# Two-layer attention trunk: softmax with queries on the partitions, scaled on GpSimd and transposed, in place of key-major scores with running sums from TensorE

## The chip, the core and the metric

The kernel runs on one core of a Trainium2 chip. The metric is the device time in microseconds (us) of one execution. The kernel before takes 1517.91 us, the median of three runs (1515.63 to 1521.51). Everything is float32; the large products are made of two or three TensorE passes over a "high" part (the value rounded to the fp32r format) and a "low" part (the rest).

## The reference

Two layers over 640 tokens (128 context tokens, tile 0, and 512 latent tokens, tiles 1 to 4), width 1024. Per layer one input projection feeds three branches; the outputs are projected, gated, merged, projected again and normalised. The change touches the attention of branches A and B only. Both have 8 query heads and 2 key/value heads of 64 columns.

```python
def dense_gqa(q, k, v, n_kv, sink=None):          # branch A; latent queries see 4 latent tiles + 1 cached tile
    s = einsum('bqkgd,blkd->bkgql', q * d**-0.5, k)
    ...                                            # branch B: the sink is one more column of s
    p = softmax(s, axis=-1)                        # without the sink's column afterwards
    return einsum('bkgql,blkd->bqkgd', p, v)

def window_gqa(q, k, v, k_ctx, v_ctx, sink):       # branch B; |i - j| <= 128, plus the cached tile, plus the sink
    s_band = where(valid, einsum(q, kband), -1e30)
    p = softmax(concatenate([s_band, s_ctx, s_sink], -1), -1)
    return p_band @ vband + p_ctx @ v_ctx
```

Context queries (tile 0) see context keys alone.

## The kernel before

**Groups and steps.** Attention runs group by group. A group is one key/value head with one tile of 128 queries, so 4 query heads and 512 (head, query) columns; `GROUPS` lists 10 of them, the context tile last. A step is one key tile of a group. Branch A has 8 groups of 5 steps and 2 of one step, 42 in all. Branch B has groups of 3 or 4 key tiles and one more step for the sink (`SINK`), 40 steps in all, 30 of them with keys. There are two layers, so 144 steps with keys and 20 with the sink.

**What a group does.** First it needs the row maximum of each query. `S` (L1043, L1045) forms the scores with queries on the partitions, one head at a time over all its latent keys in one bank (128 x 512 or 128 x 384; in B with a mask product, L1050), and the cached tile of branch A in one more unit with the four heads side by side. VectorE takes the maxima (L1586, L1589), combines them with each other or the sink (L1595 to L1602). `row` (L1057) transposes the 128 x 4 maxima; VectorE writes them, negated, into rows 96 to 99 of a copy `q_m` of the queries (L1612, L1614). Then each step `ST` forms the scores again, this time with keys on the partitions: L1071, and L1072, in which rows 96 to 99 of `k_lo` hold ones so that the maximum is subtracted inside the product; in B a mask product (L1076) where the tile needs it. ScalarE takes the exponential from the bank (L1296) and rounds it to `p_hi` (L1298), GpSimd makes `p_lo` (L1792). `PV` adds three products (L1092, L1093, L1095) to the output bank: high values times `p_hi`, low values times `p_hi`, high values times `p_lo`. The stationary tile of values is 64 columns of values next to 64 columns of ones, so the other half of the bank gathers the sum of the exponentials. For the sink, `ST` writes a diagonal tile of exponentials (L1291) and `PV` multiplies it with ones (L1089, L1095). `O` (two halves) takes the reciprocal of 64 x 256 sums (L1633) and multiplies (L1636, twice). `og`, `oh`, `ol` apply the gate and split the result (L1798, L1311, L1803).

**Order.** All engines walk one list, `ORDER`, each in its own program order, and wait on semaphores. `attention()` writes the list for a branch: a step, the `S` units and `row`s of later groups spread between, the `PV` of three steps back, and a chunk of filler: gate products over 640 tokens (L910) that do not depend on the attention. In A the filler is the gate tiles `z` 2 to 7, in 8 chunks each of 6 matmuls of 320 columns; in B it is `c` and `u`, 6 chunks each of 8 matmuls. In B `c` goes through ScalarE with Silu, which needs another table than Exp. `S` and `row` share banks 0 and 1, `ST` banks 2 and 3, `O` banks 4 and 5, filler banks 6 and 7. `with_splits` puts the preparation of weight tiles between: ScalarE rounds one (L1138), GpSimd makes its low part (L1764).

**Buffers that the change touches.** `p_f`, `p_hi`, `p_lo` (three buffers of 128 x 512 each), `o_inv`, `q_m`, `es_d`, `es_f`, `top_r`, and `vv`, the values with their columns of ones.

## Time and profile before

| | us |
|---|---|
| median of 3 runs | 1517.91 |
| the profiled execution, its own time | 1520.94 |
| its span, first to last instruction | 1519.1 |
| TensorE busy in the span | 1445.8 |
| VectorE, ScalarE, GpSimd busy | 796.1, 587.9, 771.7 |
| mean granted TensorE clock | 0.986 |

TensorE has work for all but 73.3 us of the span. A matmul's duration on the page includes its way through the pipe, so the durations of neighbours overlap; what one costs is the distance between two starts, which the timeline gives. PE stands for TensorE, PEld for its weight loads, DVE for VectorE, ACT for ScalarE, POOL for GpSimd. Line numbers are those of the kernel before.

### The profile page before, as it was taken

Reading aid. Unit: us, or ns where it says so; the run is one execution under the profiler, and the core shown is the slowest. Engines: PE = TensorE matmul, PEld = TensorE weight load, DVE = VectorE, ACT = ScalarE, POOL = GpSimd, SP = SyncE. Lnnn points to the kernel's source line nnn. Section 1 sums busy time; section 2 is a strip of 40 time slices with the busy share of each in tenths; the row PEclk is TensorE's granted clock in tenths of the full one; section 3 lists DMA queues with packets and bytes.
Section 4 is the critical chain, followed back from the end, with each engine's and each line's share of the span. In section 5 each row is a group of like instructions: output and inputs, shape, how many; then the busy total and the mean of one; then the engine's idle time right before and its main releaser. Section 6 shows DMA issues by size and latency. Waiting matters only on the chain.

```text
span 1519.1 us, 21747 instructions
## 1 busy us (share of the span) xinstructions
PE 1445.8 (95%) x8776; PEld 1306.1 (86%) x8776; DVE 796.1 (52%) x1164; ACT 587.9 (39%) x934; POOL 771.7 (51%) x554
## 2 busy tenths in 40 slices
PE   5999999999998999999979999998999999999996
PEld 3898889889887888999868988897988879999985
DVE  4675676452677520312784747764436775022157
ACT  4334564233764311213243346542357632222140
POOL 2454676323676443344674557753246755443443
PEclk9999999999999999999999999999999999999998
DMA  8412000212000443444320220012110013215221
GB/s 336 126 56 74 29 28 21 90 47 83 28 29 28 132 156 122 141 159 139 124 98 28 88 70 15 29 56 73 56 57 28 29 53 113 76 62 198 96 99 70
DMA packets 36756, 126.90 MB, mean 84 GB/s; under 512 B 5040, under 2 KB 5680, under 8 KB 36656
## 3 DMA queue, kind: packets, MB, share of 16 engines
q1 hardware_dynamic: 29952, 108.54, 21.3%
q10 hardware_dynamic: 6704, 16.97, 3.1%
q8 instruction: 70, 1.15, 0.3%
q14 instruction: 30, 0.25, 0.1%
HBM read 119.73 MB, written 5.77 MB: 83 GB/s over the span
## 4 chain that ended last, share of the span: by engine, by line
PE 87%; DVE 5%; POOL 3%; issue 2%; ACT 2%; DVEq 0%; POOLq 0%; ACTq 0%
PE ps L910 46%; PE ps L858 7%; PE ps L860 7%; PE ps L859 7%; PE ps L1045 3%; PE ps L1043 2%; PE ps L1095 2%; PE ps L1072 2%; PE ps L1071 2%; PE ps L1092 2%; PE ps L1093 2%; PE ps L927 1%; POOL w_lo L1764 1%; DVE o_inv L1633 1%; PE ps L1102 1%
## 5 line engine op out<-in xcount | busy, mean ns | idle before, releaser
L1764 POOL TENSOR_TENSOR w_lo<-raw,w_hi 128x1024 fp32r<-128x1024 f32 x148 | 360.1, 2440 | 359.0 <-ACT w_hi L1138 358.7
L910 PE MATMUL ps<-h_hi,w_hi 128*128 128x320 f32 x1280 | 299.3, 315 | 18.4 <-DVE g_c L1645 8.0
L910 PE MATMUL ps<-h_hi,w_lo 128*128 128x320 f32 x1280 | 292.6, 310 | 0.0
L910 PE MATMUL ps<-h_lo,w_hi 128*128 128x320 f32 x1280 | 292.6, 310 | 0.0
L1792 POOL TENSOR_TENSOR p_lo<-p_f,p_hi 128x512 fp32r<-128x512 f32 x164 | 211.9, 1296 | 139.0 <-ACT p_hi L1298 138.2
L910 PEld LDWEIGHTS ps<-h_hi,w_hi 128*128 128x128 f32 x1280 | 217.3, 189 | 39.3 <-DVE g_c L1645 9.8
L910 PEld LDWEIGHTS ps<-h_lo,w_hi 128*128 128x128 f32 x1280 | 215.9, 189 | 2.2
L910 PEld LDWEIGHTS ps<-h_hi,w_lo 128*128 128x128 f32 x1280 | 215.6, 189 | 2.2
L1138 ACT ACTIVATE w_hi<-raw 128x1024 fp32r<-128x1024 f32 x148 | 152.8, 1051 | 92.1 <-DMA raw<-in_weights 53.7
L1589 DVE TENSOR_REDUCE top<-ps 128x1 f32<-128x512 f32 (+1 forms) x128 | 83.7, 658 | 144.7 <-PE ps L1050 105.0
L1660 DVE TENSOR_TENSOR gy<-ps,sg 128x640 f32<-128x640 f32 x32 | 26.4, 824 | 241.2 <-PE ps L910 241.1
L1633 DVE RECIPROCAL o_inv<-ps 64x256 f32<-64x256 f32 x80 | 140.2, 1752 | 15.3 <-PE ps L1095 10.4
L1296 ACT ACTIVATE p_f<-ps 128x512 f32<-128x512 f32 x144 | 86.1, 598 | 133.0 <-PE ps L1095 117.8
L858 PE MATMUL ps<-w_hi,h_hi 128*128 128x512 f32 (+1 forms) x360 | 130.5, 362 | 4.0 <-POOL w_lo L1764 2.6
L860 PE MATMUL ps<-w_hi,h_lo 128*128 128x512 f32 (+1 forms) x360 | 128.5, 357 | 0.0
L859 PE MATMUL ps<-w_lo,h_hi 128*128 128x512 f32 (+1 forms) x360 | 128.4, 357 | 0.0
L1336 ACT ACTIVATE sg<-ps,pack 128x640 f32<-128x640 f32 x32 | 25.4, 795 | 207.7 <-PE ps L910 207.6
L1298 ACT ACTIVATE p_hi<-p_f 128x512 fp32r<-128x512 f32 x164 | 103.7, 632 | 5.2
L910 PE MATMUL ps<-o_hi,w_hi 128*128 128x320 f32 x384 | 91.4, 320 | 6.9 <-DVE rot_s L1385 6.0
L1807 POOL TENSOR_TENSOR merge<-merge,gy 128x640 f32<-128x640 f32 x32 | 51.2, 1601 | 82.3 <-DVE gy L1660 82.3
L910 PE MATMUL ps<-o_lo,w_hi 128*128 128x320 f32 x384 | 88.6, 312 | 0.0
L910 PE MATMUL ps<-o_hi,w_lo 128*128 128x320 f32 x384 | 88.6, 312 | 0.0
(180 smaller groups left out, 2599.2 us busy)
## 6 DMA issues: line engine op xcount, KB each, us to landing
raw<-in_weights SPq DMA_DIRECT2D x190, 512.0 KB, 3.4
raw_more<-in_weights SPq DMA_DIRECT2D x10, 512.0 KB, 10.6
x<-in_x_sample ACTq DMA_DIRECT2D x6, 512.0 KB, 8.0
x_mid<-x ACTq DMA_DIRECT2D x5, 512.0 KB, 2.6
x<-x_mid ACTq DMA_DIRECT2D x5, 512.0 KB, 6.5
y_sample<-x SPq DMA_DIRECT2D x3, 512.0 KB, 2.6
pack<-in_pack ACTq DMA_DIRECT2D x2, 528.0 KB, 4.8
x<-in_x_sample SPq DMA_DIRECT2D x2, 512.0 KB, 4.9
```

The lines of the kernel that those rows point to most:

```text
L858: pe.matmul(out, st_hi, mv_hi, start=start, stop=False)
L859: pe.matmul(out, st_hi, mv_lo, start=False, stop=False)
L860: return pe.matmul(out, st_lo, mv_hi, start=False, stop=stop)
L910: last = pe.matmul(ps[:, s + half, 0:HALF], w[:, u % RING, cols], acts[:, k, half * HALF:(half + 1) * HALF], start=k == 0 and part == 0, s ...
L1138: did(act.activation(w_hi[:, n % RING, :], raw_tile(r), ACT.Copy), hi_made)
L1296: did(act.activation(p_f[:, n % 3, :], ps[:, s, :], ACT.Exp), drained[s])
L1298: did(act.activation(p_hi[:, n % 3, :], p_f[:, n % 3, :], ACT.Copy), p_hi_made)
L1589: did(dve.tensor_reduce(top[:, c, 0, i:i + 1], ps[:, s, 0:n * P], axis=AX.X, op=ALU.max), drained[s])
L1633: after(did(dve.reciprocal(o_inv[0:HD, cols], ps[sums, b, cols])))
L1764: did(pool.tensor_tensor(w_lo[:, n % RING, :], raw_tile(r), w_hi[:, n % RING, :], ALU.subtract), w_ready)
L1792: did(pool.tensor_tensor(p_lo[:, n % 3, :], p_f[:, n % 3, :], p_hi[:, n % 3, :], ALU.subtract), p_lo_made)
L1807: did(pool.tensor_tensor(merge[:, j, :], merge[:, j, :], gy[:, j % 2, :], ALU.add), merged)
```

## The change

Scores are formed once, with queries on the partitions (`S`). ScalarE takes the exponential of a whole head directly from that bank, with the negated maximum as the per-partition bias, and has the row sum accumulated at the same time (`ex`); the sink becomes one more exponential of a 128 x 1 column. VectorE adds the partial sums and takes the reciprocal of a 128 x 1 column (`iv`), GpSimd multiplies the head's row of exponentials by it. The step is now `T`: four transposes of 128 x 128 on TensorE. ScalarE rounds the transposed bank to `p_hi`, VectorE makes the low part (`pl`). `PV` has two products: the stationary tile of values is 64 high columns next to 64 low columns, so the upper half of the bank gathers the low part; ScalarE copies it out and VectorE adds both (`O`, once per group). The steps of the sink, the second scores, `row`, `q_m` and the columns of ones are gone; so is row 96 to 99 of `k_lo` (the scores take 96 rows). In branch A the cached unit comes first and is copied to `cached`. `p_f` holds two whole groups. The lag from step to `PV` is 2, not 3; the filler of A begins one `z` tile earlier and eight chunks of it stand between the first `S` units, in B one gate tile of `b` is filler too. A split is held back between the last `S` of a group and its last `iv`.

```diff
+def p_place(g):
+    return (g % 2, 0, g - 2) if g < 2 * T - 2 else (0, g - (2 * T - 2), 2 * T - 4)
...
-def attention(l, br, filler, last_filler, lag, row_ahead, score_ahead):
+def attention(l, br, first_filler, filler, last_filler, lag, ahead):
...
+        holder = p_place(g)[2]
+        start = -1 if holder < 0 else first[holder + 1] - 1
+        end = max(first[g] - ahead, start)
+        ahead_of_heads = len(units) > GRP and holder >= 0
         for i, e in enumerate(units):
+            n = i - ahead_of_heads
+            at = start - 1 if n < 0 else start + (end - start + 1) * n // (len(units) - ahead_of_heads)
+            scores[at].append(e)
+            exps[at].append(("ex", *e[1:]))
+            if score_units(br, g)[e[4]] != "cache":
+                inverses[at if at < 0 else at + 1].append(("iv", *e[1:]))
...
     for n, (g, i) in enumerate(steps):
-        out.append(("ST", l, br, g, i))
-        out.extend(early[n])
+        out.append(("T", l, br, g, i))
+        out.extend(scores[n])
+        out.append(("pl", l, br, g, i))
+        out.extend(inverses[n])
         tick()
         if n >= lag:
             product(n - lag)
         fill()
+        out.extend(exps[n])
...
-    out.extend(flat(attention(l, "a", filler[:-5], filler[-5:], 3, 2, 4)))
+    out.extend(flat(attention(l, "a", filler[:8], filler[8:-5], filler[-5:], 2, 3)))
...
-    out.extend(flat(attention(l, "b", filler[:-3], filler[-3:], 3, 2, 4)))
+    out.extend(flat(attention(l, "b", filler[:9], filler[9:-3], filler[-3:], 2, 3)))
...
+        def p_part(br, g):
+            buf, behind, _ = p_place(g)
+            n = len(group_slots(br, g)) * P
+            return by_head(p_f[br][:, buf, behind * BW:behind * BW + GRP * n])
...
@@ TensorE
-                        pe.matmul(ps[:, s, :], k_hi[:, kv, key], q_t[:, heads, tokens], start=True, stop=False)
-                        last = pe.matmul(ps[:, s, :], k_lo[0:TOP_ROW + GRP, kv, key], q_m[0:TOP_ROW + GRP, n % 3, :],
-                                         start=False, stop=mask is None)
...
+                        pe.wait_ge(over_sum, NO[("iv", *e[1:4], len(score_units(br, g)) - 1)] + 1)
+                        for h in range(GRP):
+                            last = pe.transpose(ps[:, s, h * P:(h + 1) * P], p_part(br, g)[:, h, i * P:(i + 1) * P], ident)
...
-                            high, low = v_blocks(slot_key, kv)
-                            pe.matmul(ps[:, b, :], high, p_hi[:, n % 3, :], start=i == 0, stop=False)
-                            pe.matmul(ps[:, b, :], low, p_hi[:, n % 3, :], start=False, stop=False)
-                        pe.wait_ge(p_lo_made, n + 1)
-                        last = pe.matmul(ps[:, b, :], high, p_lo[:, n % 3, :], start=False, stop=ends)
+                        wait_drained(pe, ("T",) + e[1:])
+                        values = vv[:, key, kv, :, :].rearrange("p s d -> p (s d)")
+                        pe.matmul(ps[:, b, :], values, p_hi[:, n % 3, :], start=i == 0, stop=False)
+                        last = pe.matmul(ps[:, b, :], values, p_low(br, n), start=False, stop=ends)
@@ ScalarE
+                    elif kind == "ex":
...
+                        act.wait_ge(neg_made, NEG_NO[scores])
+                        if unit == "cache":
+                            did(act.activation(cached[:, g % 2, :], ps[:, s, :], ACT.Copy), drained[s])
+                            continue
+                        for h in range(GRP) if unit == "heads" else (unit,):
+                            p, bias = p_part(br, g)[:, h, :], neg[:, c % 3, h:h + 1]
+                            if br == "b":
+                                head = GROUPS[g][0] * GRP + h
+                                act.activation(sums[:, c % 3, 1, h:h + 1], sink[:, head:head + 1], ACT.Exp, bias=bias)
+                            if br == "a" and unit != "heads":
+                                wait_drained(act, ("S", l, br, g, 0))
+                                act.activation(p[:, LAT * P:], cached[:, g % 2, h * P:(h + 1) * P], ACT.Exp, bias=bias,
+                                               accum_out=sums[:, c % 3, 1, h:h + 1])
+                                p = p[:, 0:LAT * P]
+                            n = p.shape[-1]
+                            src = ps[:, s, h * P:(h + 1) * P] if unit == "heads" else ps[:, s, 0:n]
+                            last = act.activation(p, src, ACT.Exp, bias=bias, accum_out=sums[:, c % 3, 0, h:h + 1])
+                        did(last, drained[s])
@@ VectorE, S
+                            h, n = unit, len(group_slots(br, g)) - (br == "a")
+                            after(did(dve.tensor_reduce(best[:, h:h + 1], ps[:, s, 0:n * P], axis=AX.X, op=ALU.max)))
+                            other = others[:, h:h + 1] if br == "a" else sinks[:, h:h + 1]
+                            did(dve.tensor_scalar(neg[:, c, h:h + 1], best[:, h:h + 1], other, -1.0, ALU.max, ALU.mult), neg_made)
+                    elif kind == "iv":
...
+                            after(did(dve.tensor_tensor(total, total, sums[:, c, 1, heads], ALU.add)))
+                        did(dve.reciprocal(inv[:, c, heads], total), inv_made)
+                    elif kind == "pl":
...
+                        did(dve.tensor_tensor(p_low(br, n), ps[:, s, :], p_hi[:, n % 3, :], ALU.subtract), drained[s])
...
-                        after(did(dve.reciprocal(o_inv[0:HD, cols], ps[sums, b, cols])))
...
+                            last = dve.tensor_tensor(half, by_head(ps[0:HD, b, :])[:, odd:GRP:2, :], half, ALU.add)
@@ GpSimd
-                        did(pool.tensor_tensor(p_lo[:, n % 3, :], p_f[:, n % 3, :], p_hi[:, n % 3, :], ALU.subtract), p_lo_made)
+                    elif kind == "iv":
...
+                        pool.wait_ge(inv_made, NO[e] + 1)
+                        did(pool.tensor_tensor(part, part, inv[:, c, heads].unsqueeze(2).to_broadcast(list(part.shape)), ALU.mult),
+                            over_sum)
```

TensorE, one step in the middle of branch A, before: second scores (L1071, L1072), first scores of one head of a later group (L1043, L1045), three value products, one chunk of filler.

```order
L1071 MATMUL ps<-q_t,k_hi 128x512
L1072 MATMUL ps<-q_m,k_lo 128x512
L1043 MATMUL ps<-k_hi,q_t 128x512
L1045 MATMUL ps<-k_lo,q_t 128x512
L1092 MATMUL ps<-p_hi,vv 128x512
L1093 MATMUL ps<-p_hi,vv 128x512
L1095 MATMUL ps<-p_lo,vv 128x512
L910 MATMUL ps<-h_hi,w_hi 128x320 x2
L910 MATMUL ps<-h_lo,w_hi 128x320 x2
L910 MATMUL ps<-h_hi,w_lo 128x320 x2
```

The same place now: the four transposes of `T` stand where the second scores were, and one value product is gone. (The line numbers are those of the new file: L1059 and L1061 are the scores, L924 the filler.)

```order
L1075 MATMUL ps<-ident_r,p_f_a 128x128 x4
L1059 MATMUL ps<-k_hi,q_t 128x512
L1061 MATMUL ps<-k_lo,q_t 128x512
L1086 MATMUL ps<-p_hi,vv 128x512
L1087 MATMUL ps<-p_lo_a,vv 128x512
L924 MATMUL ps<-h_hi,w_hi 128x320 x2
L924 MATMUL ps<-h_lo,w_hi 128x320 x2
L924 MATMUL ps<-h_hi,w_lo 128x320 x2
```

Per group of branch A the first list runs five times before, with the scores of the cached tile as eight products of 128 columns in one of the five, and the second list runs five times now.

VectorE over about one group of branch A, before: maxima (L1586, L1589), their combination (L1600), the copy `q_m` (L1612, L1614), and twice a reciprocal with its two products (L1633, L1636).

```order
L1589 TENSOR_REDUCE top<-ps 128x1
L1586 TENSOR_REDUCE top<-ps 128x4
L1600 TENSOR_TENSOR top_r<-top 128x4
L1589 TENSOR_REDUCE top<-ps 128x1
L1612 COPY q_m<-q_t 64x512
L1614 SCALAR_TENSOR_TENSOR q_m<-ps,ident_r 4x512
L1589 TENSOR_REDUCE top<-ps 128x1
L1633 RECIPROCAL o_inv<-ps 64x256
L1636 TENSOR_TENSOR o_sum<-ps,o_inv 64x128 x2
L1589 TENSOR_REDUCE top<-ps 128x1
L1633 RECIPROCAL o_inv<-ps 64x256
L1636 TENSOR_TENSOR o_sum<-ps,o_inv 64x128 x2
```

VectorE now, from the `iv` of a group's third head over the cached tile of the group after it: sum and reciprocal of a head (L1610, L1611), `O` (L1624), the maximum of a unit (L1591, L1600) and its negation (L1602), and `pl` (L1616).

```order
L1610 TENSOR_TENSOR sums<-sums 128x1
L1611 RECIPROCAL inv<-sums 128x1
L1624 TENSOR_TENSOR o_sum<-ps,o_sum 64x256 x2
L1591 TENSOR_REDUCE top<-ps 128x4
L1616 TENSOR_TENSOR p_lo_a<-ps,p_hi 128x512
L1610 TENSOR_TENSOR sums<-sums 128x1
L1611 RECIPROCAL inv<-sums 128x1
L1600 TENSOR_REDUCE top<-ps 128x1
L1602 TENSOR_SCALAR neg<-top 128x1
L1616 TENSOR_TENSOR p_lo_last<-ps,p_hi 128x512
```

The last pair L1610, L1611 of the piece belongs to the fourth head; it stands behind the maximum of the cached unit and one `pl`, and GpSimd's multiplication of that head, on which the first `T` of the group waits, follows it.

On ScalarE the table loads of the whole program go from 28 to 32.

## Rows read from the trace of the kernel before

**Rows 1.** The page: busy time of each engine; the chain by engine.

```profile
PE 1445.8 (95%) x8776; PEld 1306.1 (86%) x8776; DVE 796.1 (52%) x1164; ACT 587.9 (39%) x934; POOL 771.7 (51%) x554
PE 87%; DVE 5%; POOL 3%; issue 2%; ACT 2%; DVEq 0%; POOLq 0%; ACTq 0%
```

**Rows 2.** Groups by line, PE: count | busy us, mean ns | idle before.

```profile
...
L1071 PE MATMUL ps<-q_t,k_hi 128*128 128x512 f32 x144 | 56.9, 395 | 0.0
L1072 PE MATMUL ps<-q_m,k_lo 100*128 100x512 f32 x144 | 57.8, 402 | 0.0
L1093 PE MATMUL ps<-p_hi,vv 128*128 128x512 f32 x144 | 56.7, 394 | 0.0
...
L1076 PE MATMUL ps<-mask_r,ident_r 128*128 128x512 f32 x24 | 9.7, 406 | 0.0
...
L1089 PE MATMUL ps<-p_hi,one_row 128*128 128x512 f32 x20 | 8.6, 430 | 0.0
```

**Rows 3.** Timeline, PE, branch A: start us, us, what.

```profile
239.44 0.39 PE L1071 MATMUL ps<-q_t,k_hi 128*128 128x512 f32 x1
...
240.60 0.45 PE L910 MATMUL ps<-h_hi,w_hi 128*128 128x320 f32 x2
...
241.47 0.39 PE L1071 MATMUL ps<-q_t,k_hi 128*128 128x512 f32 x1
```

**Rows 4.** Timeline, PE: same step, two groups apart.

```profile
193.59 0.39 PE L1071 MATMUL ps<-q_t,k_hi 128*128 128x512 f32 x1
...
218.84 0.39 PE L1071 MATMUL ps<-q_t,k_hi 128*128 128x512 f32 x1
```

**Rows 5.** Timeline, PE: four transposes of a query tile.

```profile
322.29 0.60 PE L1022 MATMUL ps<-ident_r,q_st 128*128 128x128 f32 x4
322.64 0.54 PE L910 MATMUL ps<-o_hi,w_hi 128*128 128x320 f32 x2
323.02 0.46 PE L910 MATMUL ps<-o_lo,w_hi 128*128 128x320 f32 x2
```

**Rows 6.** Windows, branches A, B: us, PE PEld DVE ACT POOL busy, PEclk.

```profile
145.00:230.00 85.00, 85.00 (x469) 74.37 (x468) 60.71 (x89) 50.66 (x83) 61.66 (x50) 1.00 0.08 26
357.00:485.00 128.00, 119.65 (x668) 106.78 (x667) 82.46 (x123) 80.92 (x147) 81.13 (x61) 0.97 0.13 42
```

**Rows 7.** Groups by line and form, DVE.

```profile
L1633 DVE RECIPROCAL o_inv<-ps 64x256 f32<-64x256 f32 x80 | 140.2, 1752 | 15.3 <-PE ps L1095 10.4 <-POOL o_lo L1803 2.6
L1589 DVE TENSOR_REDUCE top<-ps 128x1 f32<-128x512 f32 x96 | 66.0, 691 | 69.5 <-PE ps L1045 37.7 <-PE ps L1050 30.1
```

**Rows 8.** One line, DVE (ns min/median/max); timeline, POOL and DVE.

```profile
L1597 DVE TENSOR_TENSOR es_d<-pack,top_r x20: 161/660/2261, 365.5 to 1220.5; 128x4 f32<-128x4 f32 x20
...
231.24 0.74 POOL L1798 TENSOR_TENSOR o_sum<-o_sum,g_t 128x256 f32<-128x256 f32 x1
231.42 0.58 DVE L1602 TENSOR_SCALAR top_r<-top 128x4 fp32r<-128x4 f32 x1
...
461.84 2.42 POOL L1764 TENSOR_TENSOR w_lo<-raw,w_hi 128x1024 fp32r<-128x1024 f32 x1
462.12 2.16 DVE L1595 TENSOR_TENSOR top_r<-top,pack 128x4 fp32r<-128x4 f32 x1
```

**Rows 9.** Groups by line and form, ACT.

```profile
...
L1296 ACT ACTIVATE p_f<-ps 128x512 f32<-128x512 f32 x144 | 86.1, 598 | 133.0 <-PE ps L1095 117.8 <-PE ps L1072 7.3 <-POOL p_lo L1792 5.9
L1291 ACT ACTIVATE p_f<-ident_r,es_f 128x128 f32<-128x128 f32 x80 | 25.6, 390 | 16.2 <-issue 9.7 <-POOL p_lo L1792 3.8 <-PE ps L1095 2.7
L1336 ACT ACTIVATE sg<-ps,pack 128x640 f32<-128x640 f32 x32 | 25.4, 795 | 207.7 <-PE ps L910 207.6
```

**Rows 10.** Groups by line and form, POOL.

```profile
L1764 POOL TENSOR_TENSOR w_lo<-raw,w_hi 128x1024 fp32r<-128x1024 f32 x148 | 360.1, 2440 | 359.0 <-ACT w_hi L1138 358.7
...
L1807 POOL TENSOR_TENSOR merge<-merge,gy 128x640 f32<-128x640 f32 x32 | 51.2, 1601 | 82.3 <-DVE gy L1660 82.3
```

**Rows 11.** Timeline, PE, end of branch B: wait in brackets.

```profile
478.08 0.90 PE L910 MATMUL ps<-h_hi,w_hi 128*128 128x320 f32 x2 [4.12 <-DVE g_c L1645]
```

More of the change, by code:

```diff
@@ L38 @@
 CACHE = T
-SINK = T + 1
+TOP_ROW = 96
 KEY_TILES = T + 2
@@ L42 @@
 FRONT = 0
-TOP_ROW = 96
 HF_ACT = 4
@@ L289, in layer_order @@
                 ("qt", l, "b", 0)])
-    for c in range(KT_B):
+    for c in range(KT_B - 1):
         out.extend(whole(gate("b", c)))
@@ L393, in with_splits @@
 def with_splits(order, freed, lag):
-    count, out, due, turn, started = len(freed), [], {}, RING, False
+    count, out, due, turn, started, held = len(freed), [], {}, RING, False, False
     for e in order:
@@ L1590, in _ @@
[L1590 to L1603 removed]
+                        best, others = top[:, c, 0, :], top[:, c, 1, :]
```

309 lines of the change are left out of this document (120 added, 189 removed).

## The prediction

> **What bounds the kernel now.** I read the page first: TensorE is busy for 95% of the span and carries 87% of the chain that ended last [rows 1]. So work taken from TensorE is worth its full time wherever the other engines keep up. I then asked the windows whether they do: in branch A, TensorE is busy for all of 85 us, VectorE for 60.7, ScalarE for 50.7, GpSimd for 61.7; the 128 us of branch B have 119.7, 82.5, 80.9 and 81.1 [rows 6]. The others have room, 24 us of 85 on VectorE and GpSimd, and it is that room that the change spends. Last came the groups by line, for counts, and the timeline, for what one instruction costs.
>
> **TensorE, removed.** The durations of neighbours overlap, so I take starts: five products of 512 columns (L1071, L1072, L1092, L1093, L1095) start at 239.44 and what follows them at 240.60, so one costs 0.232 [rows 3]. Gone are 144 of L1071, 144 of L1072, 144 of L1093 (the third value product), 24 masks, and the sink's 20 and their 20 twins [rows 2]: 496 x 0.232 = 115 us. The 40 transposes of the maxima add about 2.
>
> **TensorE, added.** 144 steps of four 128 x 128 transposes of float32 tiles. The trace has the same thing for the queries: four of them start at 322.29, the next matmul at 322.64, and its pair then takes 0.38 until the next start instead of 0.29, so four cost 0.35 to 0.44 [rows 5]. I take 0.44, which holds the exposed weight load: 63.4 us. Net: 115 + 2 - 63.4 = **54 us less** for TensorE, 11 per layer in A (42 steps x (3 x 0.232 - 0.44)), the rest in B.
>
> **Branch A, is the room enough?** One group took 25.25 / 2 = 12.6 us [rows 4]. TensorE now needs 12.6 - 5 x 0.70 + 5 x 0.44 = 11.3, and 0.8 more because 43 chunks of filler (0.87 us each, 240.60 to 241.47 [rows 3]) stand in 42 steps and no longer in 50 places: 12.1. Filler is moved, not added. The others, per group of five steps:
> - VectorE: five maxima at 0.69 [rows 7] and five `pl`, which read the same 512 columns of a bank and are priced alike; with gaps 7.2. Four negations, four sums and four reciprocals of one column: a small operation takes 0.16 where nothing holds it [rows 8], so 2.2 with gaps. `O` is two additions of 256 columns, 0.42 each as an estimate from 0.69 for 512: 0.85. Together 10.2. Gone are the 80 reciprocals of 1.75 us [rows 7], 140 us in all; that is what pays for this.
> - ScalarE: four heads, each 0.39 for the cached 128 columns and, for 512 with a bias, between 0.60 and 0.80, say 0.69 [rows 9]: 4.3 in all. Five `p_hi` from the bank at 0.60, the cached copy 0.6, two halves of `O` 0.8, `oh` 0.4, weights and `z` 1.1: 10.2. What the accumulated sum costs no row shows. Its lower bound is nothing, its upper one a small instruction of its own, 0.39 by the smallest full-height exponential of the rows; I take 0.1, since nothing but one column is written: 11.0.
> - GpSimd: four multiplications of 128 x 640, at 1.60 like the sum over the same shape [rows 10], 6.4; `og` and `ol` 0.74 each [rows 8], 1.5; 5/8 of a weight tile at 2.44 [rows 10], 1.5. Together 9.4.
>
> So three engines need 10.2 to 12.1 and TensorE 12.1. A chain runs through all of them once per group. The last `S` of a group ends 0.9 us into its step; maximum and negation 0.9, exponentials 1.1, then `iv`, which stands behind the next unit's maximum and a `pl` on VectorE, so not before 5.2; sum and reciprocal 0.4, multiplication 1.6, at about 7.3. The first `T` of that group comes after three steps, 7.2. It is late by a few tenths each time, and `T`, the next `S`, `PV` and filler are queued behind it on TensorE. Together with three engines near their limits in fixed orders I expect 12.9 per group, 0.8 x 8.4 groups = 6.7 us per layer, and 1.5 where the branch starts, since `T` 0 waits for four multiplications in a row: 16.4 over both layers.
>
> **Branch B.** The step is longer (1.4 chunks of 8/6 x 0.87 = 1.16 us), the heads are shorter, and sinks cost one 128 x 1 exponential. I charge 3 us per layer for waits at the start and behind the table loads on ScalarE, four more in the program than before: 6. On the other side, at the end of B TensorE waited 4.12 us for the drain of a `u` tile behind VectorE's reciprocals [rows 11], once per layer; with these gone I count 5 us back for both. The two memsets dropped ahead of branch A give 1.5.
>
> **Sum:** 1520.9 - 54 + 16.4 + 6 - 5 - 1.5 = 1483 for an execution like the profiled one. That one stood 3.0 above the median of the runs, so the same difference of 38 us from the median gives **1480 us**.
>
> **A wait that may decide branch A.** While GpSimd ran `w_lo` from 461.84 to 464.26, an addition of four columns on VectorE, started at 462.12, took 2.16 us, to 464.28. While it ran `og` from 231.24, the one `tensor_scalar` of this kind, started at 231.42, took 0.58, to 232.00, where `og` ended at 231.98 [rows 8]. Small operations on SBUF operands wait for GpSimd's whole instruction: L1597 has 0.16 at best, 0.66 in the median [rows 8]. The new `iv` sum is such an operation, and GpSimd is about to be busy with the multiplication that the last `iv` released. In the forecast 1.65 us lie between a reciprocal and the next sum, about one multiplication, so it costs little. The negation, one column, comes 0.7 us after the reciprocal. Whether one column waits too, no row shows; from below it is 0.16, from above the rest of a multiplication, 0.9 more.
>
> The Trainium skill, SBUF — State Buffer, section "Who interferes with whom", has this as a rule: VectorE with two SBUF inputs, or in a two-port mode, is blocked for the whole GpSimd instruction. By that rule the trace agrees (2.16 us behind `w_lo`). Its Vector Engine (DVE) Microarchitecture Reference, section 5.1, lets `tensor_scalar` into the two-port mode also with an odd count, if source and output match. One column would then be held, which speaks against my 12.9 and for the first rival; no row here has one column.
>
> **Rivals.**
> 1. The negation is held. Then a loop closes: reciprocal, multiplication (1.7), negation 0.2, `pl` 0.7, sum and reciprocal 0.4, that is 3.0 us for each of two steps, 2.5 for the first head, 2.9 for the second with `O`, 2.1 at the cached tile: 13.5 per group, whatever TensorE saves. For it: the 0.58 us row. Against it: that row had four columns. Price: 1.4 x 8.4 + 3 at the start = 15 per layer in A and 6 in B: -60.5 + 42, so **1500**.
> 2. Slower. The same loop, but with the rest of GpSimd's queue inside it, since a weight tile or `og` or `ol` stands ahead of a multiplication: 13.5 + 1.5 + 1.5 = 16.4 per group if all of it falls into the loop. Price: 36 + 3 per layer in A, 10 in B: -60.5 + 98, so **1555**. It decides from 14.6 per group on. Against it: the splits are held back around a group's last head, and part of the queue runs while VectorE works.
> 3. Nothing stalls that does not stall now: 1517.9 - 60, **1458**. For it: the sums above are all below 12.1. Against it: the late first `T`.
> 4. ScalarE becomes the bound: the accumulation costs 0.35 us and not 0.1. Then 10.2 + 8 x 0.35 = 13.0, and with gaps some 14 per group: 1.9 x 8.4 + 1.5 and 6 in B per layer, -60.5 + 47, so **1505**. For it: no row prices it. Against it: only one column is written.
>
> **Chances.** Forecast 54% (its own range 1465 to 1497), rival 1 18%, rival 2 12%, rival 3 8%, rival 4 8%. The range of 8 in 10 reaches from 1457 to 1520. What a measurement of this kernel can tell from no change is about 0.5%, 7.6 us. Below 1510.3 lie the forecast, rival 3, nearly all of rival 1 and most of rival 4: 79%. Above 1525.5 lies rival 2 with a little of the others: 13%. Between: 8%.
>
> **What would show it.** Starts of `T` transposes: 0.44 per four. The stride of a group of branch A: 12.9 is the forecast, 12.1 rival 3, 13.5 rival 1, above 14.6 rival 2. The negation of one column: at 0.16 to 0.2 rival 1 and 2 are dead; with a median near 0.9 and ends at the ends of GpSimd's multiplications they live. The exponentials of 512 columns: at 0.7 to 0.8 the forecast, near 1.05 rival 4. GpSimd's multiplication should take 1.6; a broadcast operand that made it 2.9 would bind the branch by itself (4 x 2.9 + 3 = 14.6). The forecast is wrong if TensorE waits in branch A for VectorE's `pl` or for a bank of `S` in every step and not only at the first `T` of a group, or if its granted clock falls below the 1.00 of now [rows 6] there.

## The result and the profile after

The changed kernel takes 1471.45 us (median of 4 runs, 1470.61 to 1475.29), the kernel before 1518.42 (4 runs). The ratio is 0.9695, with a 95% interval of 0.9669 to 0.9721: 47 us less, where 38 were forecast. The time lies in the forecast's range and in the likeliest case's own range; it is 9 us below the number.

First the page of the kernel after: its span, the busy time of each engine, and the chain by engine.

```profile
span 1470.1 us, 22567 instructions
...
PE 1392.7 (95%) x8816; PEld 1276.4 (87%) x8816; DVE 726.2 (49%) x1412; ACT 638.3 (43%) x1298; POOL 704.0 (48%) x520
...
PE 79%; DVE 4%; POOL 3%; ACT 2%; issue 2%; DVEq 0%; POOLq 0%; ACTq 0%
```

Against [rows 1], TensorE's busy time fell from 1445.8 to 1392.7 us, by 53.1; the sum had 54. Its idle time is the span less its busy time: 1519.1 - 1445.8 = 73.3 before, 77.4 now. It rose by 4.1, where the other terms of the sum (+16.4 + 6 - 5 - 1.5) make 15.9. So the whole miss lies in the waits, and the waits are the next view to read. Columns: who waited, for what, us in total, times, the longest.

```profile
PE ps L1075 <- POOL p_f_a L1772: 5.4, 4, 2.4
PE ps L1059 <- ACT p_f_b L1292: 4.2, 6, 1.0
PE ps L924 <- DVE g_c L1632: 3.6, 4, 0.9
PE ps L1075 <- DVE p_lo_a L1616: 3.0, 2, 1.5
...
PE ps L1059 <- ACT p_f_a L1292: 1.9, 2, 1.4
...
PE ps L924 <- ACT g_c L1329: 1.6, 2, 0.8
```

The same view of the kernel before, the rows that answer to two of these:

```profile
PE ps L910 <- DVE g_c L1645: 8.0, 4, 4.1
...
PE ps L910 <- ACT g_c L1322: 6.0, 8, 1.8
```

Two things are to be seen. The new waits of branch A are 5.4 + 3.0 + 1.9 = 10.3 us, and there are eight of them in the whole program, four per layer: TensorE doesn't wait once per group, it waits twice at the start of the branch and in two places behind it. And two old waits shrank, from 8.0 to 3.6 and from 6.0 to 1.6.

What a step of branch A looks like, on TensorE's timeline. Columns: start us, us, engine, line, what.

```profile
190.03 0.60 PE L1075 MATMUL ps<-ident_r,p_f_a 128*128 128x128 f32 x4
190.38 0.48 PE L1059 MATMUL ps<-k_hi,q_t 128*128 128x512 f32 x1
190.70 0.39 PE L1061 MATMUL ps<-k_lo,q_t 96*128 96x512 f32 x1
190.94 0.39 PE L1086 MATMUL ps<-p_hi,vv 128*128 128x512 f32 x1
191.17 0.39 PE L1087 MATMUL ps<-p_lo_a,vv 128*128 128x512 f32 x1
191.40 0.45 PE L924 MATMUL ps<-h_hi,w_hi 128*128 128x320 f32 x2
...
192.26 0.60 PE L1075 MATMUL ps<-ident_r,p_f_a 128*128 128x128 f32 x4
...
197.21 0.60 PE L1075 MATMUL ps<-ident_r,p_f_a 128*128 128x128 f32 x4
...
208.92 0.60 PE L1075 MATMUL ps<-ident_r,p_f_a 128*128 128x128 f32 x4
```

Four transposes take 0.35 to the next start, and the product behind them takes 0.32 instead of 0.23: 0.44 per four, as taken from [rows 5]. From 197.21 to 208.92 is one group: 11.7 us, with TensorE never idle. By the forecast it was 12.9, and 12.1 where TensorE alone sets it. The forecast had the first `T` of a group a few tenths late behind GpSimd's multiplication for the fourth head. That multiplication and that `T`:

```profile
197.76 1.25 POOL L1772 TENSOR_TENSOR p_f_a<-p_f_a,inv 128x640 f32<-128x640 f32 x1 [1.25 <-DVE inv L1611]
...
199.48 0.60 PE L1075 MATMUL ps<-ident_r,p_f_a 128*128 128x128 f32 x4
```

The step with the last `S` of this group started at 192.26. The multiplication ends at 199.01, 6.75 us behind it (the forecast had 7.3), and `T` follows at 7.22 (the forecast had 7.2): 0.47 us to spare. At the forecast's price of 1.60 for the multiplication 0.12 would be left.

The windows of the two branches (columns as in [rows 6]):

```profile
145.00:230.00 85.00, 80.90 (x530) 74.45 (x529) 65.97 (x161) 65.65 (x184) 51.77 (x43) 1.00 0.09 32
346.00:474.00 128.00, 122.91 (x774) 114.64 (x773) 70.37 (x192) 89.70 (x209) 72.02 (x66) 1.00 0.17 58
```

In branch A ScalarE rose from 50.7 to 65.7 of 85 us and VectorE from 60.7 to 66.0; GpSimd fell from 61.7 to 51.8. TensorE lost 4.1 of 85 us there, nearly all of it in two places. The timeline of all engines around them, the idle time before an instruction in brackets:

```profile
181.20 2.38 POOL L1749 TENSOR_TENSOR w_lo<-raw,w_hi 128x1024 fp32r<-128x1024 f32 x1
181.35 2.25 DVE L1610 TENSOR_TENSOR sums<-sums 128x1 f32<-128x1 f32 x1
...
183.71 0.86 DVE L1624 TENSOR_TENSOR o_sum<-ps,o_sum 64x256 f32<-64x256 f32 x2
...
184.61 0.69 DVE L1591 TENSOR_REDUCE top<-ps 128x4 f32<-128x512 f32 x1
185.34 0.69 DVE L1616 TENSOR_TENSOR p_lo_a<-ps,p_hi 128x512 fp32r<-128x512 f32 x1
...
186.37 1.25 POOL L1772 TENSOR_TENSOR p_f_a<-p_f_a,inv 128x640 f32<-128x640 f32 x1 [1.24 <-DVE inv L1611]
...
187.77 0.63 PE L1075 MATMUL ps<-ident_r,p_f_a 128*128 128x128 f32 x4 [2.37 <-POOL p_f_a L1772]
...
223.72 2.39 POOL L1749 TENSOR_TENSOR w_lo<-raw,w_hi 128x1024 fp32r<-128x1024 f32 x1
223.72 2.41 DVE L1597 TENSOR_SCALAR neg<-top 128x4 f32<-128x4 f32 x1
226.05 0.68 DVE L1616 TENSOR_TENSOR p_lo_a<-ps,p_hi 128x512 fp32r<-128x512 f32 x1
...
226.78 0.66 PE L1075 MATMUL ps<-ident_r,p_f_a 128*128 128x128 f32 x4 [1.50 <-DVE p_lo_a L1616]
```

The one-column sum starts 0.15 us after GpSimd's `w_lo` and ends with it, after 2.25 us instead of 0.15. Everything on VectorE is late by that; GpSimd sits idle until the inverse comes; the transposes wait 2.37. That is the loop of rival 2, closed once. The second layer has the same wait (2.38 us, ended at 913.65). The second place is its twin: the four-column negation of the cached part, started with another `w_lo`, takes 2.41, and TensorE waits 1.50 for the `p_lo` behind it. So 3.9 of these 4.1 us are VectorE operations of a few columns behind a weight split.

The small forms, each as one line of the kernel (ns min/median/max) or as a group by form (busy us, mean ns):

```profile
L1602 DVE TENSOR_SCALAR neg<-top x64: 212/214/215, 129.3 to 945.0; 128x1 f32<-128x1 f32 x64
...
L1772 POOL TENSOR_TENSOR p_f_a<-p_f_a,inv 128x640 f32<-128x640 f32 x64 | 80.2, 1253 | 74.4 <-DVE inv L1611 74.4
...
L1292 ACT ACTIVATE p_f_a<-ps,neg 128x512 f32<-128x512 f32 x64 | 43.2, 675 | 0.1
...
L1292 ACT ACTIVATION_READ_ACCUMULATOR p_f_a<-ps,neg 128x1 f32 x80 | 15.7, 196 | 0.0
```

The negation of one column is never held: 59 of the 128 in both branches started while GpSimd had at least 0.4 us of an instruction before it, and the longest of them took 217 ns. The reciprocals of one column (128, 162 to 168 ns) were not held either. The multiplication takes 1.25, not 1.60. The exponential takes 0.675 (0.69 was taken), and its sum is a second instruction of 0.19.

### The profile page after: what moved, and what is told of

Same layout as the page of the kernel before. It is cut to its first block, busy times and chain, and to the rows that moved or that the text cites. A ratio compares the mean times of both kernels' runs of the same rounds, so it can differ in the third digit from the quotient of the medians.

```text
span 1470.1 us, 22567 instructions
## 1 busy us (share of the span) xinstructions
PE 1392.7 (95%) x8816; PEld 1276.4 (87%) x8816; DVE 726.2 (49%) x1412; ACT 638.3 (43%) x1298; POOL 704.0 (48%) x520
## 4 chain that ended last, share of the span: by engine, by line
PE 79%; DVE 4%; POOL 3%; ACT 2%; issue 2%; DVEq 0%; POOLq 0%; ACTq 0%
PE ps L924 45%; PE ps L872 6%; PE ps L874 6%; PE ps L873 6%; PE ps L1075 4%; PE ps L1059 3%; PE ps L1061 2%; PE ps L1086 2%; PE ps L1087 2%; POOL w_lo L1749 1%; PE ps L941 1%; ACT p_f_a L1292 1%; PE ps L1094 1%; POOL p_f_a L1772 1%; PE ps L1066 1%
## 5 line engine op out<-in xcount | busy, mean ns | idle before, releaser
L924 PE MATMUL ps<-h_hi,w_hi 128*128 128x320 f32 x1280 | 298.1, 314 | 11.5 <-DVE g_c L1632 3.6
L924 PE MATMUL ps<-h_lo,w_hi 128*128 128x320 f32 x1280 | 293.0, 310 | 0.0
L924 PE MATMUL ps<-h_hi,w_lo 128*128 128x320 f32 x1280 | 292.9, 310 | 0.0
L924 PEld LDWEIGHTS ps<-h_hi,w_hi 128*128 128x128 f32 x1280 | 218.0, 189 | 31.5 <-issue 9.1
L924 PEld LDWEIGHTS ps<-h_hi,w_lo 128*128 128x128 f32 x1280 | 215.7, 189 | 1.7
L924 PEld LDWEIGHTS ps<-h_lo,w_hi 128*128 128x128 f32 x1280 | 215.3, 188 | 1.6
L1600 DVE TENSOR_REDUCE top<-ps 128x1 f32<-128x512 f32 (+1 forms) x128 | 83.9, 655 | 111.3 <-PE ps L1066 78.1
L1772 POOL TENSOR_TENSOR p_f_a<-p_f_a,inv 128x640 f32<-128x640 f32 (+1 forms) x68 | 84.3, 1241 | 80.4 <-DVE inv L1611 80.4
L1772 POOL TENSOR_TENSOR p_f_b<-p_f_b,inv 128x512 f32<-128x512 f32 (+1 forms) x68 | 62.9, 940 | 77.6 <-DVE inv L1611 77.6
L1303 ACT ACTIVATE p_hi<-ps 128x512 fp32r<-128x512 f32 x144 | 85.6, 594 | 31.8 <-PE ps L1075 28.4
L924 PE MATMUL ps<-o_hi,w_hi 128*128 128x320 f32 x384 | 91.4, 320 | 6.9 <-DVE rot_s L1392 6.0
L924 PE MATMUL ps<-o_lo,w_hi 128*128 128x320 f32 x384 | 88.7, 312 | 0.0
L924 PE MATMUL ps<-o_hi,w_lo 128*128 128x320 f32 x384 | 88.5, 312 | 0.0
L1059 PE MATMUL ps<-k_hi,q_t 128*128 128x128 f32 (+2 forms) x224 | 81.6, 381 | 7.2 <-ACT p_f_b L1292 4.2
## 6 DMA issues: line engine op xcount, KB each, us to landing
raw_more<-in_weights SPq DMA_DIRECT2D x10, 512.0 KB, 10.6
```

The source lines that it names most:

```text
L924: last = pe.matmul(ps[:, s + half, 0:HALF], w[:, u % RING, cols], acts[:, k, half * HALF:(half + 1) * HALF], start=k == 0 and part == 0, s ...
L1059: pe.matmul(ps[:, s, col:col + width], q_t[:, head, t * P:(t + 1) * P], k_hi[:, kv, src], start=True, stop=False)
L1303: did(act.activation(p_hi[:, n % 3, :], ps[:, s, :], ACT.Copy), p_hi_made)
L1600: after(did(dve.tensor_reduce(best[:, h:h + 1], ps[:, s, 0:n * P], axis=AX.X, op=ALU.max)))
L1772: did(pool.tensor_tensor(part, part, inv[:, c, heads].unsqueeze(2).to_broadcast(list(part.shape)), ALU.mult), over_sum)
```

## The experiments

Twelve kernels ran. Each ratio is to the kernel before on the same chip (1518.8 to 1520.3 us there); "after" is 1471.45 throughout.

### What is TensorE's time worth?

`third_product`: one more product of 512 columns per step.

```diff
                        pe.matmul(ps[:, b, :], values, p_hi[:, n % 3, :], ...)
+                       pe.matmul(ps[:, b, :], values, p_hi[:, n % 3, :], start=False, stop=False)
```

> The changed kernel with one more product per group of values (values by p_hi a second time, so that the output holds that part twice): 144 products of 512 columns. My theory: TensorE's time sets the end and a column that is taken away or added is worth its full time, 144 x 0.232 = 33 us, so about 1505 us, busy TensorE time up by 33 and its idle time unchanged within 5. The rival, that the loop of VectorE, ScalarE and GpSimd sets the pace of branch A: the products fill idle time there, and the kernel comes out at 1472 to 1485.

1493.56 us (ratio 0.9826, 0.9809 to 0.9842): 22 us more, between the two. Its page:

```profile
span 1493.8 us, 22855 instructions
...
PE 1422.2 (95%) x8960; PEld 1300.4 (87%) x8960; DVE 726.4 (49%) x1412; ACT 639.6 (43%) x1298; POOL 704.2 (47%) x520
```

Busy time rose by 29.5, 0.205 per product. The price of 0.232 itself holds where the clock is the same (two of these products start at 192.17 and 192.41 on this run's timeline); most of the difference is the mean granted clock, 0.989 here and 0.987 in the changed kernel, by estimate 0.002 x 1400 = 3 us. Idle time fell by 5.8, to 71.6 (waits for `p_f_a` out of GpSimd from 5.4 to 3.6, for example). So a product put in is worth 22 / 144 = 0.15, two thirds of the 0.232 that I gave it.

`before_two_products`, the opposite from the other side:

```diff
-                            pe.matmul(ps[:, b, :], low, p_hi[:, n % 3, :], start=False, stop=False)
```

> The kernel before without its third product (low values by p_hi, left out of the result): 144 products of 512 columns. Theory: a product that is taken away is worth its time while TensorE hardly waits: 144 x 0.232 = 33 us, 1519 - 33 = 1486. The rival: the other engines then set the pace of branch A in the old order and give back a third or more of it, 1495 or above.

1493.93 us (0.983, 0.9813 to 0.9847): 25 us less. It lies between the two, 8 us above the theory and one below the rival's bound of 1495; 8 of 33 us were given back, a quarter and not a third. TensorE's busy time fell by 31.1 and its idle time rose by 5.7. But that isn't the rival's mechanism: the waits that grew most are those for VectorE's `g_c`, from 8.0 to 10.6, and for ScalarE's, from 6.0 to 7.8, and they stand in branch B. In branch A it is chiefly the waits for `p_lo` that grew, from 0.4 to 1.6. So of the 47 us, this one product brings 25 if it alone is taken out of the kernel before, and costs 22 if it is put back into the changed one; the other 22 to 25 came with the exchange of the scores.

### Why were the waits smaller than forecast?

`before_copied_sums`: the reciprocal of 64 x 512 sums in the kernel before becomes a copy.

```diff
-                        after(did(dve.reciprocal(o_inv[0:HD, cols], ps[sums, b, cols])))
+                        after(did(dve.tensor_copy(o_inv[0:HD, cols], ps[sums, b, cols])))
```

> The kernel before with the reciprocal of 64 x 512 sums out of PSUM (1.75 us, 80 of them) replaced by a copy of the same form (the division is left out). Theory: VectorE's long reciprocals cost TensorE only at the end of branch B, where the transposes wait for g_c for 4.1 us, twice for 8.0 in all with the shorter ones, so 5 us come back: 1514. The rival: the reciprocals hold up nothing, or the copy takes as long as they did: 1519. A third reading, that they hold up branch A too, would give 1505 or less.

1512.05 us (0.9951, 0.9936 to 0.9966): 7 us less. VectorE lost 107 us of its 140 on that line. Among TensorE's waits for the attention and its filler only one row moved much (a wait that ends at 21.6 us, long before the attention, went from 2.5 to 0.5 too):

```profile
PE ps L910 <- ACT g_c L1322: 6.0, 8, 1.7
...
PE ps L910 <- DVE g_c L1645: 2.1, 4, 0.8
```

So the reciprocals held TensorE up at the end of branch B and nowhere else, as the prediction had it; the wait fell by 5.9 us, in all of the program. The clock adds to it. TensorE's windows of the kernel before, around that wait (it ended at 478.08, [rows 11]):

```profile
478.00:482.60 4.60, 4.52 (x14) 4.15 (x15) 0.30 (x2) 0.23 (x1) 2.44 (x2) 0.50 0.21 60
482.60:487.00 4.40, 4.40 (x28) 4.18 (x28) 4.24 (x6) 3.22 (x8) 1.75 (x2) 0.98 0.15 61
```

For 4.6 us after the 4.12 us stall the granted clock was 0.50, the lower of the two levels (1.2 GHz), and as many matmuls took twice as long: about 2.3 us on top of the stall, which my 5 left out. This isn't so each time: behind the same wait of the second layer (3.48 us, ended at 1228.6) the clock stayed at 1.00. The wait for ScalarE's `g_c`, on the other hand, stayed at 6.0 here and fell to 1.6 in the changed kernel, so it was not the reciprocals that made it; what did was not tested.

`full_operand`, `added_scale` and `other_tile` ask what GpSimd's instruction costs, and whether its price has a part in the miss. One line each:

```diff
-  did(pool.tensor_tensor(part, part, inv[:, c, heads].unsqueeze(2).to_broadcast(list(part.shape)), ALU.mult), ...)
+  did(pool.tensor_tensor(part, part, part, ALU.mult), ...)                            # full_operand
+  did(pool.tensor_tensor(part, part, inv[...].to_broadcast(...), ALU.add), ...)       # added_scale
+  part = part.rearrange("p h (a b) -> p (h a) b", b=P)                                # other_tile
+  did(pool.tensor_tensor(part, part, other_tile[:, :, :].to_broadcast(list(part.shape)), ALU.mult), ...)
```

> The changed kernel with GpSimd multiplying the exponentials by themselves in place of the inverse sums (the scaling is left out; the second operand is then a full 128 x 640 tile, where it was four columns spread over it). Theory: the multiplication takes 1.25 us instead of the 1.60 that I took from a row of before because its second operand is small; here it goes back to 1.60 for 640 columns, and since the multiplication still has room in GpSimd's share of a group (9.4 of 11.7 us by my sum) the kernel loses 0 to 5 us. The rival: 1.60 belonged to the other operation and this one takes 1.25 here as well, with no change of the total.

> The changed kernel with GpSimd adding the inverse sums to the exponentials where it multiplied them (the result is then another; sizes and operands are the same). full_operand showed that the second operand's size does not matter. Theory: GpSimd's addition costs more than its multiplication: 1.60 us for 640 columns, as the additions of this size to merge take, against 1.25; and as 4 x 0.35 = 1.4 us more of GpSimd's time per group of branch A (1.25 in branch B for 512 columns) leave it below TensorE's 12.1, the kernel loses 3 to 10 us: 1475 to 1481. That would be the share of my forecast's excess that lies in this price. The rival: an addition on this tile takes 1.25 as well, and merge is slow for another reason: 1471.

> The changed kernel with GpSimd multiplying the exponentials by another tile of constants (128 columns of 0.5, read again for each 128 columns of exponentials; the scaling by the sums is left out). The multiplication took 1.25 us for 640 columns with the four inverse sums as second operand and with the exponentials themselves (full_operand), and so did the addition (added_scale), where the addition of gy to merge took 1.60 us for the same size. What is left that differs: there the two operands are different full streams. Theory: with such a second stream it takes 1.60 here, 4 x 0.35 = 1.4 us more per group of branch A; GpSimd stays below TensorE, and the kernel takes 1471 to 1477, so that the price of the multiplication has no part in the excess of my forecast. The rival: it takes 1.25 again, and the price hangs on where the tiles lie or on what runs beside them; 1471.

1470.97 us (0.9675, 0.9661 to 0.9689), 1471.73 (0.9687, 0.967 to 0.9705) and 1475.64 (0.9708, 0.9686 to 0.973). GpSimd's group by form, one row out of each kernel in this order:

```profile
L1772 POOL TENSOR_TENSOR p_f_a<-p_f_a 128x640 f32<-128x640 f32 x64 | 80.2, 1254 | 72.1 <-DVE inv L1611 72.1
```

```profile
L1772 POOL TENSOR_TENSOR p_f_a<-p_f_a,inv 128x640 f32<-128x640 f32 x64 | 80.2, 1253 | 76.0 <-DVE inv L1611 76.0
```

```profile
L1775 POOL TENSOR_TENSOR p_f_a<-p_f_a,other_tile 128x640 f32<-128x640 f32 x64 | 100.2, 1566 | 57.0 <-DVE inv L1612 57.0
```

Both of my first theories fell (the operand's size; multiplication against addition). The third held: with another tile as second stream it takes 1.57, with the same tile, or with one column per head, 1.25. And at 1.57 the kernel is 4 us slower, within the 0 to 6 expected; the intervals of the two ratios (0.9669 to 0.9721 for after) overlap, so that even this is not certain. TensorE's waits for `p_f_a` out of GpSimd are then seven and 7.1 us, against four and 5.4: the forecast's late first `T` begins to show (0.17 us at 161.74), but is far from 0.8 per group. The price of the multiplication explains little of the miss, since GpSimd was not at its limit.

### Which small operation is held?

`sum_by_scalar`: the sum of one column plus one column written in the form of the negation.

```diff
-                        if br == "b" or unit != "heads":
+                        if unit != "heads":
+                            after(did(dve.tensor_scalar(total, total, sums[:, c, 1, heads], None, ALU.add)))
+                        elif br == "b":
```

> The changed kernel with the one-column sum of two ScalarE totals (128 x 1 plus 128 x 1) written as an addition of a per-partition scalar, the form of the negation. In the changed kernel the sum with two tile inputs took 2.25 us once per layer, beside GpSimd's w_lo of 2.38, and the transposes behind it waited 2.4 us. Theory: it is the two-input form that GpSimd holds; in the other form it takes 0.2 us always, the 2.4 us stall goes, and with it 2 layers x 2.4 = about 5 us: 1467. The rival: the transposes wait there for ScalarE or for GpSimd's own w_lo, the multiplication is late in any case, and the total doesn't move.

1464.26 us (0.9639, 0.9619 to 0.9659); its five runs (1462.76 to 1469.60) all lie below the lowest of the changed kernel. The line of the sum, and the same place of the timeline:

```profile
L1610 DVE TENSOR_SCALAR sums<-sums x128: 193/204/215, 133.9 to 1163.7; 128x1 f32<-128x1 f32 x128
...
183.23 2.40 POOL L1751 TENSOR_TENSOR w_lo<-raw,w_hi 128x1024 fp32r<-128x1024 f32 x1
183.33 0.20 DVE L1610 TENSOR_SCALAR sums<-sums 128x1 f32<-128x1 f32 x1
...
188.19 0.63 PE L1075 MATMUL ps<-ident_r,p_f_a 128*128 128x128 f32 x4 [0.83 <-POOL p_f_a L1774]
```

The sum starts 0.1 us after the same `w_lo` and takes 0.20; the wait behind it is 0.83 instead of 2.37. The theory holds: it was the form with two tile inputs that was held. The size is less plain: this place gives 2 x 1.5 = 3 us, the span of the profiled execution is 3.2 less (its time, 1469.04, is among the upper ones of the five), and the medians differ by 7.2. Much of the rest goes with the clock: the three executions from 1462.8 to 1464.3 had a mean granted clock of 0.991, the two at 1469 had 0.989 and 0.987, and those of the changed kernel 0.985 to 0.988. A difference of 0.003 over 1391 busy us is, by estimate, 4 us. A part of that belongs to the stalls, since one of the two was followed by a slow clock (shown below); how large a part these runs don't tell.

`neg_two_columns` and `neg_three_columns` put the hold where rival 1 had it:

```diff
-        neg = sb("neg", [P, 3, GRP])
+        neg = sb("neg", [P, 3, GRP, 2])                                # 3 in neg_three_columns
...
-  did(dve.tensor_scalar(neg[:, c, h:h + 1], best[:, h:h + 1], other, -1.0, ALU.max, ALU.mult), neg_made)
+  did(dve.tensor_scalar(neg[:, c, h, :], best[:, h:h + 1].to_broadcast([P, 2]), other, -1.0, ALU.max, ALU.mult), neg_made)
```

> The changed kernel with the negation of branch A's maximum written on two columns instead of one (the same value twice; ScalarE reads the first). In the changed kernel all 128 of them took 0.21 us, those beside a multiplication of GpSimd too, while the form over four columns is held (0.45 on average, up to 2.4). If an even number of columns is what lets GpSimd hold it (the condition of my rival 1), they go to between 0.6 and 1.6 us where a multiplication runs, ScalarE's exponentials come later, and a group of branch A takes 13.5 instead of 11.7 us: 1485 to 1500 us. If the form is never held when it reads and writes so few columns: 0.22 us each and 1471.

> As neg_two_columns (1490.8 us; the negation took 0.53 and 0.70 us on average and was held until GpSimd's multiplication ended), with three columns in place of two. If an odd count of columns is what keeps GpSimd from holding it: 0.22 us each and 1471 us. The rival, that one column is a case of its own and any wider write is held: 0.5 to 0.7 us and 1491, as with two.

1490.83 us (0.9812, 0.9793 to 0.9831) and 1496.19 (0.9844, 0.9819 to 0.987): 19 and 25 us more than after. (The 0.45 for the four-column form in the first expectation is its median; its mean is 0.87.) The timeline of `neg_two_columns`:

```profile
178.28 1.25 POOL L1772 TENSOR_TENSOR p_f_a<-p_f_a,inv 128x640 f32<-128x640 f32 x1 [1.24 <-DVE inv L1611]
178.83 0.73 DVE L1602 TENSOR_SCALAR neg<-top 128x2 f32<-128x2 f32 x1
179.49 0.73 POOL L1779 TENSOR_TENSOR o_sum<-o_sum,g_t 128x256 f32<-128x256 f32 x1
...
193.95 0.63 PE L1075 MATMUL ps<-ident_r,p_f_a 128*128 128x128 f32 x4 [2.38 <-POOL p_f_a L1772]
```

The negation ends where the multiplication does (179.56 against 179.53). The group of `neg_three_columns` by form shows the same: mean 551 ns, against 214.

```profile
L1602 DVE TENSOR_SCALAR neg<-top 128x3 f32<-128x3 f32 x64 | 35.2, 551 | 2.3
```

So it is not the odd count: one column is free, two and three are held. Rival 1's consequence came too, at its price of 20 us (1500 against 1480): the hold costs 19. The span of the profiled execution is 23.0 us longer (1493.1): 12.1 are idle time of TensorE and 10.9 busy time, at an unchanged 8816 instructions. The clock again (0.981 on average against 0.987, by estimate 8 of the 10.9 us), in windows of `neg_two_columns` before and after the end of the 2.38 us wait at 193.95:

```profile
190.00:194.00 4.00, 1.62 (x10) 1.25 (x10) 3.83 (x9) 1.17 (x3) 2.70 (x3) 1.00 0.39 133
194.00:198.00 4.00, 4.00 (x17) 3.57 (x18) 2.16 (x6) 3.03 (x10) 1.13 (x2) 0.57 0.01 4
```

The 2.37 us wait of the changed kernel was followed by no such fall (1.00 in the window [145:230] above), but its twin of 2.38 us in the second layer of the same execution was. The window of `after` behind it:

```profile
913.60:917.60 4.00, 3.95 (x16) 3.56 (x17) 1.74 (x6) 2.72 (x8) 1.24 (x2) 0.58 0.00 0
```

So a stall of this length can cost its 2.4 us alone or some 1.7 more (4 us at 0.57 or 0.58), in the same kernel at the same place of its two layers.

### Did ScalarE bound it?

`no_sum`, and `no_sum_scalar` on top of `sum_by_scalar`:

```diff
-  last = act.activation(p, src, ACT.Exp, bias=bias, accum_out=sums[:, c % 3, 0, h:h + 1])
+  last = act.activation(p, src, ACT.Exp, bias=bias)
```

> The changed kernel without the row sums of ScalarE's exponentials (the division by them is left out: they are ones). In the changed kernel each of the 224 exponentials is followed by a read of its total, 0.19 us, 43 us of ScalarE in all, which I had taken at 0.1 each inside the exponential. Theory: ScalarE isn't what sets the pace of a group (11.7 us, of which it works some 9), so the total falls by 0 to 5 us, to 1467 to 1471. The rival (my rival 4), that ScalarE bounds branch A: 8 x 0.19 = 1.5 us per group come back, 16 groups, about 24 us: 1447.

> The changed kernel with the sum as a scalar addition (1464.3 us) and without the row sums of the exponentials (the division is left out), as in no_sum (1460.5). It separates the two effects in no_sum. Theory: most of what no_sum gained was the hold of VectorE's sum beside w_lo, which it shortened; then this kernel comes out within 3 us of no_sum, 1458 to 1462, and ScalarE's 224 reads of a total are worth some 4 us. The rival, that the reads' 43 us on ScalarE cost 11 us by themselves: 1453.

1460.50 us (0.9611, 0.9595 to 0.9627) and 1459.86 (0.9612, 0.9594 to 0.9631). The first was outside both expectations. The second sorts it: on top of `sum_by_scalar` the reads are worth 1464.3 - 1459.9 = 4.4 us (the intervals of the two ratios overlap a little: 0.9619 to 0.9659 and 0.9594 to 0.9631), and the two kernels are alike within 1 us. So of the 11 us of `no_sum` some 7 were, by difference, the hold, which its other timing shortened (the sum's longest there is 1.39 us instead of 2.26), with what the clock adds. 43 us of ScalarE for 4 us of time: ScalarE is not the bound.

`tables_early`, a version meant to be faster still:

```diff
+                        if unit != "cache" and ("S",) + e[1:] in FIRST_AFTER_SILU:
+                            act.activation(early[:, :], minus_half[:, 0:1], ACT.Exp)
```

> The changed kernel with the sum as a scalar addition (as in sum_by_scalar, 1464.3 us) and with a 128 x 1 exponential on ScalarE ahead of the wait of each first exponential that follows a SiLU: its table load (1.28 us) then runs while ScalarE would wait for the scores. Theory: TensorE's waits for p_f_a and p_f_b out of ScalarE are 5.9 us in all, a part of it behind a table load, so 2 to 4 us go: 1461. The rival: the loads lie beside other work and the additional exponentials cost ScalarE 13 x 0.3 = 4 us for nothing: 1464.

1463.50 us (0.9632, 0.9618 to 0.9647), against 0.9639 (0.9619 to 0.9659): no difference that can be told. The early loads did take something off in branch A: the waits for `p_f_a` out of ScalarE are 0.8, where `sum_by_scalar` has 2.8. Those for `p_f_b` are 4.6, not less than the 4.2. That is 1.6 us together, less than the runs of one kernel differ by. The best version found is `sum_by_scalar`, 1464 us.

## Why the prediction came out as it did

- **TensorE removed and added, -54.** Right: -53.1 of busy time. The price of four transposes (0.44) was right. What busy time is worth was told too simply: a product of 0.232 that was put in or taken out alone was worth 0.15 to 0.17, since waits shrank or grew against it.
- **Branch A, "three engines near their limits in fixed orders I expect 12.9 per group", 16.4 over both layers.** This term was mis-sized: 10.3 us of waits, in eight places, and 11.7 for a group that runs undisturbed. The start of the branch, 3.0 of the 16.4, took 2.5; the other 13.4 had a wait in each group, where there are two per layer, 7.8 us in all. The three sums per group (10.2, 11.0, 9.4) stood below TensorE's 12.1, and the windows bear them out or are lower: 66, 66 and 52 of 85 us. The step that failed is "late by a few tenths each time": the first `T` has 0.47 us to spare in the group shown, where the forecast had it 0.1 late; 0.35 of that difference is the multiplication, priced at 1.60 for 1.25, and TensorE waits for `p_f_a` out of GpSimd four times in the whole program, not once per group. `other_tile` shows that the price alone is worth some 4 us. What is left of the waits in A is the two held operations (3.9 us per layer) and the first exponentials. ScalarE's sum cost 0.19, not 0.1, and that didn't bind either.
- **Branch A, the 12.1 for TensorE alone.** It was 0.4 too long as well: the two groups of [rows 4] hold nine chunks of filler already, so the tenth adds 0.44 per group and not 0.8, and 11.3 + 0.4 is the 11.7 that was measured. The total doesn't hang on that, since filler is moved, not added.
- **Branch B, 6.** 4.2 us of waits for `p_f_b`.
- **The reciprocals, -5.** The mechanism was right (`before_copied_sums`), its size 7 with the slow clock behind one of the stalls; in the changed kernel 4.4 us of these waits are gone. Another 4.4 us came from waits for ScalarE's `g_c`, which the sum did not have; their cause is open.
- Together: the new waits were 14.5 us, not 22.4, and the old ones that went 8.8, not 5. That is 11.7 of the 11.8 us by which the idle time (+4.1, for +15.9) was missed. All other waits together fell by 1.6. Whether that is the memsets' 1.5 can't be told: a wait for `k_st` ahead of branch A fell from 1.9 to 0.4, but one of 1.0 for `k_lo` and one of 1.1, which the kernel before doesn't have, now stand there.
- **The number.** The time lies in the range, but the terms of the waits all erred to the same side (branch A by 6.1 us, the old waits by 3.8, branch B by 1.8) and none made up for another; the likeliest case's own range, 1465 to 1497, was wide enough for it. For branch A what happened was closer to rival 3, no wait per group, so that its result fell into the forecast's range is in part luck and doesn't bear out the account of 12.9.
- **Rival 1**: its condition was false for one column, and its loop was real: with two columns it costs what it was priced at, though part of those 19 us is the slower clock. "Whether one column waits too, no row shows" was the open question on which most of the rival's chance hung.
- **Rival 2**: its mechanism, with a weight tile inside the loop, occurs once per layer through the sum, and once more through the negation of the cached part. The first made the group from 182.98 to 197.21 14.2 us long, where the ones beside it took 11.7.
- **Rival 3** ("nothing stalls", 1458) deserved more than its 8%: the result lies 13 us above it and 9 below the forecast, and `sum_by_scalar` comes within 6 us of it.
- **Rival 4**: the read of 0.19 is a small instruction, as its upper bound had it, at half the size; no bound.
- The Trainium skill, SBUF — State Buffer, section "Who interferes with whom": the trace agrees for two SBUF inputs (the sum, 2.25 us behind `w_lo`; as `tensor_scalar` 0.20). Its Vector Engine (DVE) Microarchitecture Reference, section 5.1, with odd counts where source and output match: two and three columns are held, in line with it; one column is not (214 ns, 128 times). The page's condition is on the outermost dimension that isn't of one element, which one column lacks; I had read it as allowing the mode there, and the measurement decides against that reading.

## What to carry to other kernels

Where each engine's work per group, priced row by row, stays a tenth below the bounding engine's, as here, charge waits at the places where a pipeline starts and where a small operation can be held behind a long one, and a surcharge per group only if the chain through the engines, priced from rows, comes out clearly later than the step that needs it; 7.3 against 7.2 us was no such case. Then look at every one-column VectorE operation inside the loop beside a busy GpSimd: one column with a per-partition scalar as second operand was never held here, two tile inputs or two columns were, and such operations were worth 7 to 25 us in these runs, the clock's share included. (Four one-column negations in place of the four-column one, behind which TensorE waited 1.5 us per layer, were not tried.) A stall of TensorE by 2.4 us or more is to be priced as a range, from its length alone to some 2 us more.

## What the runs showed of the hardware

- GpSimd's two-input instruction on 128 x 640 float32 takes 1.25 us with one column per head, or with its own first operand, as second operand, and 1.57 to 1.60 with another full stream; multiplication and addition cost the same.
- ScalarE's accumulated sum is an instruction of its own (0.19 us), 224 times.
- VectorE's `tensor_scalar` with one column was held by GpSimd in none of 128 cases (212 to 217 ns, 59 of them started with 0.4 us or more of GpSimd's instruction to run); with two, three and four columns it was held until GpSimd's instruction ended (up to 2.4 us).
- After stalls of 2.4 and 4.1 us TensorE's granted clock was 0.57 and 0.50 for about 4 us, and after others of 2.4 and 3.5 us it stayed at 1.00. The two stalls of 2.4 us in the changed kernel are the same place of its two layers, one with the fall and one without. What tells these apart was not tested.
- The mean granted clock of executions of one kernel differed by up to 0.004 (`sum_by_scalar`, 0.987 to 0.991), with 1469.6 us at the one end and 1462.8 at the other.
